# A new order of transfers and matmul groups in the opening of a two-block transformer kernel

## What is computed

```
mod = silu(c) @ w_ada + b_ada                       # 2048 -> 3 * 2048
shift, scale, gate = split(mod, 3)
h = rms(x) * norm_g * (1 + scale) + shift
proj = h @ w_in                                     # 8 kinds of 1024 columns
y = concat(chunk_attention(...), hgrn2(...)) @ w_out
x = x + gate * y
...
m_k, m_v = split(rms(mem) @ w_mem_kv)               # second block's memory attention
```

## Time and profile before

| | |
|---|---|
| median of three runs | 2687.93 us |
| the profiled execution | 2686.11 us, its span 2684.8 us |
| TensorE matmul busy | 2653.0 us, 99% of the span |
| TensorE weight load | 2120.1 us, 79% |
| VectorE, ScalarE, GpSimd busy | 922.7, 1062.3, 1157.4 us |
| HBM read | 304.16 MB, 120 GB/s over the span |

### The profile page before, as it was taken

One profiled execution on the slowest core, in us unless ns is written; L12 is line 12 of the kernel. 1 busy time (PEld: TensorE's weight loads), 2 busy tenths in 40 slices (PEclk: granted clock), 3 DMA queues, 4 the chain that ended last, 5 costly groups with the idle time before them and its releaser, 6 DMA issues.

```text
span 2684.8 us, 33659 instructions
## 1 busy us (share of the span) xinstructions
PE 2653.0 (99%) x13726; PEld 2120.1 (79%) x13726; DVE 922.7 (34%) x1558; ACT 1062.3 (40%) x1716; POOL 1157.4 (43%) x587
## 2 busy tenths in 40 slices
PE   6999999999999999999999999999999999999999
PEld 4577888888888888878887777777888888888787
DVE  3536544333223221244576233234232224121400
ACT  5334444434333442244444443444443444333321
POOL 0024334343444454453344444445545556454543
PEclk9999999999999999999999999999999999999999
DMA  9942223233333224422222323332333333333343
GB/s 377 365 143 95 95 103 110 79 116 116 114 108 108 83 97 150 144 103 79 87 79 79 102 87 105 100 99 98 110 106 108 110 107 117 118 113 116 131 148 106
DMA packets 102105, 323.13 MB, mean 120 GB/s; under 512 B 11328, under 2 KB 12992, under 8 KB 101440
## 3 DMA queue, kind: packets, MB, share of 16 engines
q1 hardware_dynamic: 98208, 307.35, 33.4%
q10 hardware_dynamic: 3744, 13.63, 1.3%
HBM read 304.16 MB, written 16.78 MB: 120 GB/s over the span
## 4 chain that ended last, share of the span: by engine, by line
PE 95%; DMA 2%; DVE 2%; ACT 1%; POOL 0%; issue 0%; SPq 0%; ACTq 0%; DVEq 0%
PE bank L769 28%; PE bank L770 27%; PE bank L771 27%; PE bank L974 1%; PE bank L963 1%; DMA TA<-in_w_ada 1%; PE bank L819 1%; PE bank L674 1%; DVE Hlo L1578 1%; PE bank L957 1%; PE bank L895 1%; PE bank L928 1%; PE bank L892 1%; PE bank L1009 1%; PE bank L1023 0%; POOL wlo L2043 0%
## 5 line engine op out<-in xcount | busy, mean ns | idle before, releaser
L2043 POOL TENSOR_TENSOR wlo<-wraw,whi 128x1024 fp32r<-128x1024 f32 (+3 forms) x430 | 993.2, 2311 | 1396.3 <-ACT whi L1078 1395.9
L769 PE MATMUL bank<-Hhi,whi 128*128 128x512 f32 x2928 | 1195.2, 408 | 2.0 <-DVE par L1527 0.4
L771 PE MATMUL bank<-Hhi,wlo 128*128 128x512 f32 x2928 | 1144.5, 391 | 0.0
L770 PE MATMUL bank<-Hlo,whi 128*128 128x512 f32 x2928 | 1144.0, 391 | 0.0
L1078 ACT ACTIVATE whi<-wraw 128x1024 fp32r<-128x1024 f32 (+2 forms) x454 | 457.4, 1008 | 693.2 <-PE bank L771 671.2
L769 PEld LDWEIGHTS bank<-Hhi,whi 128*128 128x128 f32 x2928 | 550.6, 188 | 146.9 <-issue 28.3
L770 PEld LDWEIGHTS bank<-Hlo,whi 128*128 128x128 f32 x2928 | 551.3, 188 | 118.1 <-issue 10.8
L771 PEld LDWEIGHTS bank<-Hhi,wlo 128*128 128x128 f32 x2928 | 550.1, 188 | 118.5
L769 PE MATMUL bank<-Ohi,whi 128*128 128x512 f32 x320 | 128.1, 400 | 0.9 <-DVE TA L1610 0.9
L771 PE MATMUL bank<-Ohi,wlo 128*128 128x512 f32 x320 | 124.8, 390 | 0.0
L770 PE MATMUL bank<-Olo,whi 128*128 128x512 f32 x320 | 124.7, 390 | 0.0
(11 more groups left out here) (265 smaller groups left out, 2381.4 us busy)
## 6 DMA issues: line engine op xcount, KB each, us to landing
wraw<-in_w_in SPq DMA_DIRECT2D x304, 512.0 KB, 3.4
TA<-in_w_ada SPq DMA_DIRECT2D x64, 512.0 KB, 7.5
wraw<-in_w_out SPq DMA_DIRECT2D x32, 512.0 KB, 3.4
wraw<-in_w_o SPq DMA_DIRECT2D x32, 512.0 KB, 3.5
wraw<-in_w_mem ACTq DMA_DIRECT2D x16, 512.0 KB, 7.0
Y<-in_w_ada SPq DMA_DIRECT2D x16, 512.0 KB, 4.4
first<-in_w_ada SPq DMA_DIRECT2D x16, 512.0 KB, 4.4
tmp_mgs<-TA SPq DMA_DIRECT2D x32, 256.0 KB, 2.1
```

Source lines behind the costliest of these rows:

```text
L769: e.matmul(out, hi[:, c], xhi[k], start=first and j == 0, stop=False)
L770: e.matmul(out, hi[:, c], xlo[k], start=False, stop=False)
L771: m = e.matmul(out, lo[:, c], xhi[k], start=False, stop=last and end)
L2043: e.tensor_tensor(M.wlo[b][:, 0:w], M.wraw[b][:, 0:w], M.whi[b][:, 0:w].bitcast(F32), ALU.subtract).then_inc(S.lo)
```

## The change

Seven things move; no operation is added or taken away.

- `START`: six memory pieces first, then one unit after every three; the units 4 to 7 stand behind or between the last pieces and sums. Unit 8 leaves `START`.
- `BEGUN`: tiles 48 and 41 are begun one unit sooner each, and units 8 to 15 lie between the eight tiles, with 12 and 13 side by side and 14 and 15 side by side.
- TensorE's x sums go to `mem(14)`, `mem(15)`, `ada(4)`, `ada(5)`, the matmul with ones to `ada(6)`.
- ScalarE's squares go to `mem(13)`, `mem(14)`, `mem(15)`, `ada(4)`, its copy to `ada(5)` and the row to `ada(6)`.
- VectorE's `normed` goes to `ada(7)` (two times four tiles), `ada(8)` and `ada(9)`.
- SP issues the four transfers of `x` ahead of transfers 12, 13, 14 and 15 of `w_ada`.

```diff
-START = [... "m0 m1 m2 a0 m3 m4 a1 m5 m6 a2 m7 a3 m8 m9 a4 m10 s0 m11 a5 m12 a6 m13 a7 m14 s1 m15 a8"]
-BEGUN = ((48, 3, (9,)), (41, 2, (10,)), (56, 4, (11,)), (33, 5, (12,)), (49, 1, (13,)), (57, 0, (14, 15)), (40, 7, ()),
-         (32, 6, ()))
+START = [... "m0 m1 m2 m3 m4 m5 a0 m6 m7 m8 a1 m9 m10 m11 a2 m12 m13 m14 a3 m15 a4 a5 s0 a6 a7 s1"]
+BEGUN = ((48, 3, ()), (41, 2, (8,)), (56, 4, (9,)), (33, 5, (10,)), (49, 1, (11,)), (57, 0, (12, 13)),
+         (40, 7, (14, 15)), (32, 6, ()))
...
+    def x_sum(q):
+        pe.wait_ge(S.xsq, 4 * q + 4)
+        groups(M.bS0, [ones[:, 0:32]] * 4, M.xsq, q == 0, q == 3).then_inc(S.xst)
...
-        if k in (6, 8, 10, 12):
-            q = (k - 6) // 2
-            pe.wait_ge(S.xsq, 4 * q + 4)
-            groups(M.bS0, same, M.xsq, q == 0, q == 3).then_inc(S.xst)
-        if k == 13:
-            pe.wait_ge(S.xrow, 1)
-            e.matmul(M.bS0, ones, M.xsq[1], start=True, stop=True).then_inc(S.xst)
+        if k in (14, 15):
+            x_sum(k - 14)
...
+        if q in (4, 5):
+            x_sum(q - 2)
+        if q == 6:
+            pe.wait_ge(S.xrow, 1)
+            e.matmul(M.bS0, ones, M.xsq[1], start=True, stop=True).then_inc(S.xst)
...
-        if 4 <= k < 12:
-            for x in (2 * k - 8, 2 * k - 7):
-                act.wait_ge(S.x[x // 4], 16)
-                act.wait_ge(S.xst, x // 4)
-                e.activation(M.xsq[x % 4], M.y[x], ACT.Square).then_inc(S.xsq)
...
+        if k > 12:
+            x_square(k - 13)
...
+    def x_square(q):
+        for x in range(4 * q, 4 * q + 4):
+            act.wait_ge(S.x[q], 16)
+            act.wait_ge(S.xst, q)
+            e.activation(M.xsq[x % 4], M.y[x], ACT.Square).then_inc(S.xsq)
+
+    def ada(q):
+        if q == 4:
+            x_square(3)
...
-        if k in (14, 15):
-            normed(4 * k - 56)
...
-        if q in (9, 10):
-            normed(4 * q - 28)
+        if q == 7:
+            normed(0)
+            normed(4)
+        if q in (8, 9):
+            normed(4 * q - 24)
...
-            if a in (4, 6, 8, 10):
-                i = a // 2 - 2
+            if a in range(12, 16):
+                i = a - 12
```

More of the change, by code:

```diff
@@ L51 @@
 PLACES = 8
-START = [(x[0], int(x[1:])) for x in ("m0 m1 m2 a0 m3 m4 a1 m5 m6 a2 m7 a3 m8 m9 a4 m10 s0 m11 a5 m12 a6 m13 a7 "
-                                      "m14 s1 m15 a8").split()]
-BEGUN = ((48, 3, (9,)), (41, 2, (10,)), (56, 4, (11,)), (33, 5, (12,)), (49, 1, (13,)), (57, 0, (14, 15)), (40, 7, ()),
-         (32, 6, ()))
+START = [(x[0], int(x[1:])) for x in ("m0 m1 m2 m3 m4 m5 a0 m6 m7 m8 a1 m9 m10 m11 a2 m12 m13 m14 a3 m15 a4 a5 s0 "
+                                      "a6 a7 s1").split()]
+BEGUN = ((48, 3, ()), (41, 2, (8,)), (56, 4, (9,)), (33, 5, (10,)), (49, 1, (11,)), (57, 0, (12, 13)),
+         (40, 7, (14, 15)), (32, 6, ()))
 GATE_SLOTS = 6
@@ L1136, in mem @@
             e.activation(M.rr, M.rr, ACT.Exp, scale=-0.5).then_inc(S.rr)
-        if k == 12:
+        if k > 12:
+            x_square(k - 13)
+        beat.done("mem", [])
+    def x_square(q):
[6 more added lines that the diff above has]
+            x_square(3)
+        if q == 5:
             act.wait_ge(S.xst, 4)
             e.activation(M.xsq[1], M.bS0, ACT.Copy).then_inc(S.xrow)
-        if k == 13:
+        if q == 6:
             act.wait_ge(S.xst, 5)
@@ L1144, in mem @@
             e.activation(M.xr, M.xr, ACT.Exp, scale=-0.5).then_inc(S.xr)
-        beat.done("mem", [])
-    def ada(q):
         if q % 4 == 3:
```

## The result

The changed kernel takes 2695.95 us, median of 5 runs (2694.74 to 2700.27), against 2685.16 for the kernel before, median of 5; the ratio is 1.0042, with a 95% interval of 1.0031 to 1.0052. Beside the experiments it ran once more, as e8_changed_again: 2694.37 against 2686.51, ratio 1.0031 (1.0019 to 1.0042). It is slower by 8 to 11 us, 0.3 to 0.4%. The forecast was 2692.0, +4.1 us over the median known then, and had the sign, the stage and most of the mechanisms; about half of the loss or more it had not.

What follows compares the result with a forecast made beforehand. The opening alternates between DMA bandwidth (to 51 us) and TensorE's work, the eight-place ring behind. Terms -1.5, -1.6, +3.8 and waits +2.3 - 0.25 + 1.2 gave, rounded, +4.1 us: 2692.0; own range 2689.5 to 2694.5, overall 2684 to 2698.

Steps and rivals of the forecast that it cites:

- the rival's size: Opening: clock falls at unit 15, 2694.6 us, or 2696.1 with 8.5 us landings of memory pieces; chance together 0.33.
- Part 1, what is removed: Opening, memory pieces first: 7.2 us of waits on w_ada and the half clock behind unit 2's go, 9.9 us in all.
- The walk: TensorE's opening from 22.18 us: units 0, 1, 2 at 36.6, 48.5, 59.6; the 14th memory piece done at 67.4.
- Part 1, "just enough, at no cost": Opening: with 7.0 us landings memory pieces come one per 3.5 us, TensorE takes 3.6 each, so no cost.
- with 2 us to spare: Opening: late x and the last four memory pieces land by about 70 us; unit 3 is wanted at 71.8.
- My rival: Last five memory pieces, landing in 8.5 us: up to 1.5 us lost; with the clock rival, chance 0.33 together.
- part 2: x sums at m14, m15, units 4 to 6: waits for ScalarE's squares of 0.7, 0.0, 0.5, 0.6, together 1.8 us.
- Part 3, the release time: Units 4 to 7: release takes 9.8 us; waits 1.0, 0.95, 3.4 at units 5 to 7; first half tile 109.4.
- Part 4: Begun tiles: two more units, waits 2.3 at unit 13, 2.1 at 15, 1.2 at tile 40; end 168.4 against 164.24.
- units land as fast as their bytes: Rival on conditioning units in the opening: a unit lands in 7.2 us, total +1.9, 2689.8 us; chance 0.14.
- the start is cured without x in the queue: Rival at 22.18 us: the fourth w_mem piece comes in time, 2.3 us and half clock go, 2687.7; chance 0.10.
- No unit is waited for: Rival at units 5 to 7, 13, 15: five release waits, 9.75 us, go; -5.6, 2682.3 us; chance 0.10.

Runs made afterwards that it cites:

- e8_changed_again: The changed kernel itself, unaltered, run once more beside the experiments: 2694.37 us against 2686.51 for the kernel before, ratio 1.0031.
- e1: The changed kernel with x's four transfers issued where they were before, ahead of w_ada transfers 4, 6, 8 and 10: 2692.19 us, ratio 1.0018 to the kernel before.
- e7: e1 plus 6 and 9 unused matmuls ahead of TensorE's waits for units 6 and 7: 2692.11 us, ratio 1.0022 to the kernel before.
- e3: The kernel before with the changed list of begun tiles alone, unit 8 out of its opening list: 2693.85 us, ratio 1.0026.
- e10: Units spread among memory pieces, x early, squares ahead of ScalarE's split, begun list as before, unit 8 ending the opening list: 2684.92 us, ratio 0.9996 to before.

## Why the prediction was right, and where it was not

- **The stage and the sign.** That only the opening changes, and everything behind it shifts alike, holds within 1.4 us over all kernels. The change is slower than before, at the rival's size (+6.6 to +8.2) or somewhat above it, not at the forecast's +4.1. The outcome that I held most likely, within 0.2% (0.52), did not come; slower by more had 0.38. The measured 2695.95 lies in the stated range, 2684 to 2698, and above the forecast's own, 2689.5 to 2694.5. That 2692.0 comes as near as 4 us is in part luck: it was counted from 2687.93, and the five runs of before have 2685.16.
- **Part 1, what is removed.** Right: no dry spell at unit 2, the window 40:60 full. The walk holds within 1.3 us up to there: units 0, 1 and 2 at 36.18, 47.66 and 58.37, forecast 36.6, 48.5 and 59.6.
- **Part 1, "just enough, at no cost".** This step failed. I took landings of 7.0 us, measured beside an average queue, for the stretch in which the change puts x into the other queue, three of its transfers among the 5.2 MB of my own part 1; there they take 9.2 (8.2 in the repetition, by the same view). And the 5.2 MB were not hidden "with 2 us to spare": unit 3 is waited for, 0.32 to 0.36 us, in three of the four profiles with x late. My rival had 8.5 us and +1.5; in the repetition the first x sum waits 2.19 instead of the 0.7 of part 2, in the first profile 5.37 plus a half clock. The Trainium skill, DMA: Bandwidth & Descriptors, section on queues, rings and completion order, has each DMA engine take turns between the queues by packet. Half of the bandwidth for each queue, which I had made of it, would have landed the pieces sooner than 7.0: the trace disagrees, 9.2 against 7.5 with x elsewhere.
- **Part 3, the release time.** Right in kind: units 5, 6 and 7 are waited for, 0.17, 2.60 and 1.34 us in the first profile, and unit 5 2.21, unit 7 3.74 in the repetition. Too low in two terms: unit 7, with no weight piece beside it, still takes 9.9 us from the end of unit 5 in e1 (82.9 to 92.80), not 8.5; and the half clock, taken for nothing there, stretches units 5 and 7 and chunk 1's sums in the repetition (3.25, 2.43, 3.57 against 1.9 and 1.95), units 6 and 7 in the first profile. The estimate at e7 puts what of that counts at units 6 and 7 at 1.7 us; for the sums behind them, on which h waits, it counts in full, 1.6. First half tile done: 109.4 forecast, 114.10 and 118.46 measured. With x early it is 110.28 (e1) and 110.37 (e7), so all but 1 us of the 4.7 to 9.1 us by which it came late goes with x.
- **Part 4.** Right in kind: 59.0 us forecast from the first half tile to the last, 58.4 and 60.6 measured, 60.0 in e3, 61.1 in e1 and 62.8 in e7, which have the same list. Tile 40 waits 1.23 (1.2 forecast); the wait at unit 13 varies, 1.49 to 4.86 (2.3 forecast), and that at unit 15 from none to 2.58 (2.1 forecast).
- **The rivals.** That units land as fast as their bytes (7.2 us), and the estimate of 6.8 us worked out from the Trainium skill, DMA: Bandwidth & Descriptors, section on the anatomy of one DMA (on the GpSimd path), are not borne out: the units waited for in the two profiles of the changed kernel landed 8.3 us (unit 7 of the repetition) to 12.1 us (unit 13 of the first) after their release. Over units 5 to 15 of all the profiles it was 7.4 us (unit 8 of e1) to 13.6 us (unit 13 of e10), so the release time is not a fixed 9.8 us give or take 0.5, as my range had it. That the start is cured without x in the queue is out: the wait at 22.14 is 2.67, and over the seven profiles of e1's table it is 1.24 to 2.67 with x late and 1.06 to 2.63 with x early. "No unit is waited for" is out.

In sum: +4.1 forecast; late landings of the last memory pieces and of unit 5 account for 3.5 to 6.5 more by e1, of which the trace puts part into waits and part into the half clock that follows them. How the rest divides between landings and clock stays open.

## What to carry to other kernels

When transfers are moved, take the landing times of everything else in that stretch anew: a time to landing goes with what else stands in the queues, not with the transfer alone. In a ring with a release time, count the work between a user and the one two behind it; side by side costs the difference each time. And work that stands in a wait, as units 8 and 9 did in the wait for h, is free there, and costs its own time elsewhere.

## What the hardware showed unexpectedly

The time to landing of a 512 KB transfer varied with what stood in the queues (medians of a stretch). On SyncE's queue it was 3.4 us over the body of the kernel. On ScalarE's queue, from 20 to 40 us, it was 3.5 to 4.2 in the four profiles with x late, where SyncE issues nothing more until unit 0 is done, and 6.9 to 7.3 in the three with x early. From 40 to 70 us it was 7.4 to 7.6 beside w_ada alone, and 8.0 to 9.2 beside w_ada and x.

In all thirteen profiles the granted clock fell to 1.2 GHz at the sums of chunks 2 and 3, a run of 32 matmuls on one column (3.92 us in the kernel before): during that run or up to 1.2 us behind its end, with an idle time of 0.42 us in between. Which of the two the fall goes with, no run here separates.
